# The norm's scale per token moved behind the matmul, with sums and root beside the first unit of each stage

## Chip, cores and metric

One core of a Trainium2 chip runs the whole program. The metric is the device time of one execution in microseconds (us).

## The reference, cut to what matters

One inference step of a two-layer decoder trunk for 592 tokens (64 sample tokens, 16 meta tokens, a prompt of 512), D_MODEL 1024, D_FF 4096. Every sub-layer is preceded by a norm over the features:

```python
def _rmsnorm(x, g, eps=1e-6):
    xf = x.astype(jnp.float32)
    y = xf * lax.rsqrt(jnp.mean(xf * xf, axis=-1, keepdims=True) + eps)
    return (y * g.astype(jnp.float32)).astype(x.dtype)

def _sq_relu_mlp(x, w_up, w_down):
    return jnp.square(jax.nn.relu(x @ w_up)) @ w_down
...
        hp = hp + _sq_relu_mlp(_rmsnorm(hp, ln_ffn[l]), w_up[l], w_down[l])
        hs = hs + _sq_relu_mlp(_rmsnorm(hs, ln_ffn[l]), w_up[l], w_down[l])
```

(hp and hs are the prompt's and the samples' activations; the mixers stand behind a norm in the same way, and a final norm follows.) Layer 0's mixer has one input projection (24 column blocks of 128 and a small one of 140 columns), sparse attention and a gated delta rule side by side, and one output projection. Layer 1's mixer is the HGRN2 recurrence between an input projection (forget, query and gate, 24 blocks; values, 1024 columns) and an output projection. The norm's root is one number per token, so it can be applied to a product's columns as well as to the activations. In the MLP the square makes it a factor root squared on the hidden values, which again can wait until after the second product.

## The kernel before, in words

Activations lie feature-major: h, xn, x_hi and x_lo are eight tiles (k) of 128 features by 592 tokens. Weights come as units of 128x1024 (512 KB), 200 in all, through a ring of four slots that SP refills (`sp_weights`, L1944 on). Every product is made in split precision: ScalarE rounds a weight unit to w_hi (`act_w_hi`, L353), VectorE makes the rest, w_lo (`dve_w_lo`, L357); the activations are split in the same way (`act_x_hi`, L332; `dve_x_lo`, L339). `pe_unit` (L360 to 374) multiplies one unit: per tile k six matmuls of 296 columns, 48 in all, into two of four PSUM banks, so units alternate between two pairs of banks. A unit waits for its split weights and for the evacuation two units back. ScalarE and VectorE split unit j + 2 when unit j has ended.

The stages of units are: 24 of layer 0's input projection (`pe_even`, `act_even`, `dve_even`, L1405 to 1470, with the small product `pe_small`, L485, after the second unit, and the rotation of keys and queries, `pe_rope`, after units 1 to 6); attention and the delta rule; 8 of the output projection (`pe_dense`, `act_out`, `dve_out`); 64 of the first MLP (`pe_ffn`, `act_ffn`, `dve_ffn`: four steps of 8 up units and 8 down units); 24 of the odd layer's projection, evacuated by ScalarE (`act_dense`, L393); 8 of its values (`pe_values5`, L1515, tokens in rows, in all banks); the recurrence; 8 of its output projection; 64 of the second MLP; a last norm and the output's DMA.

A norm (number n, 0 to 4) stands ahead of each of the five stages of products or output. ScalarE squares tile k of h (`act_square`, L278) as soon as its residual is added, into one of two buffers; GpSimd (VectorE for n = 0) adds tiles 0 to 6 into rn (`add_squares`, L287, L290). `pe_norm` (L314) sums over features with a matrix of ones, four matmul instructions for rn and four for the last square. ScalarE takes logarithm and root (`act_root`, L301, L304). VectorE scales tile by tile (`dve_norm`, L322: h times the norm's weight times the root), alternating with x_lo, while ScalarE makes x_hi between them; the first unit takes each tile when it is there.

In the MLP VectorE evacuates: a maximum (L470) and a square (L472) for up units, `dve_residual` (L425: h plus the product) for down units and output projections.

The opening: SP's queue sends x in four parts of 592 KB, then four weight units; ScalarE's queue sends the constants (2046 KB, with the matrix of ones and the rotation tables), the vectors (57 KB, with the norms' weights) and the small product's weights (560 KB); GpSimd's queue sends the page table and the convolution's history. All engines wait for constants and vectors before they start.

Of the kernel before, what the change touches and what calls it, by code (L numbers as in the profile page):

```python
# [147 lines left out]
def hybrid_step(nc, x, consts, keep, at, w, wsmall, vecs, stconv, sdelta, shgrn, kvpages, ptab,  # L148
                y, krows, vrows, ikrows, convo_p, convo_s, delta_p, delta_s, hgrn_p, hgrn_s):
    ctx = ExitStack()  # L150
    with ctx:
# [59 lines left out]

        pages = region(B, NS * NPG, 3 * P).rearrange("p (s g) (a c) -> p s g a c", s=NS, a=3)
# [55 lines left out]
        def act_square(n, k):  # L268
            if n == 0:
                nc.scalar.wait_ge(sg(f"x_in{k * XIN // KT}"), 16)  # L270
            else:
                m0 = (Units.out_e, Units.odd - 8, M_OUT_O, UNITS - VUNITS - 8)[n - 1]
                nc.scalar.wait_ge(bank_free, m0 + k + 3)
# [6 lines left out]
        def add_squares(eng, n):  # L280
            for k in range(1, KT - 1):
                c = (KT - 2) * n + k
                eng.wait_ge(sg("norm_sq"), KT * n + k + 1)
                if k == 1:
                    if n:
                        eng.wait_ge(sg("x_f"), KT * n)
# [19 lines left out]
        def pe_norm(n):  # L306
# [3 lines left out]
            for last, v in enumerate((rn[:, :], sq[:, 1, :])):  # L310
                if last:
                    nc.tensor.wait_ge(sg("norm_sq"), KT * (n + 1))
                for e in range(2):
                    mm = nc.tensor.matmul(ps[:, 6 + e, 0:HALF], C("ones"), v[:, e * HALF:(e + 1) * HALF],  # L314
                                          start=(not last), stop=bool(last))
            mm.then_inc(sg("norm_mm"), 1)

        def dve_norm(n, dst):
            nc.vector.wait_ge(sg("norm_rt"), n + 1)
            for k in range(KT + 1):  # L320
                if k < KT:
                    ins = nc.vector.scalar_tensor_tensor(out=dst[:, k, :], in0=h[:, k, :],  # L322
                                                         scalar=vec[:, V_LN + 8 * n + k:V_LN + 8 * n + k + 1],
                                                         in1=rn[:, :], op0=ALU.mult, op1=ALU.mult)
                    ins.then_inc(sg("x_f"), 1)
                if k and n < 4:
                    dve_x_lo(dst, k - 1)


# [30 lines left out]
        def pe_unit(base, per, i, j, x, first=None):  # L360
# [5 lines left out]
            for k in range(KT):  # L366
                if first:
                    first(k)
                for a, b in ((wh, x[0]), (wh, x[1]), (wl, x[0])):
                    for e in range(2):  # L370
# [3 lines left out]
                                              stop=(k == KT - 1 and a is wl))  # L374
            mm.then_inc(w_used, 1)
# [8 lines left out]
        def pe_dense(groups, u0, n):  # L384
            with nc.tensor.Fori(0, groups) as i:
# [1852 lines left out]
```

## Time and profile before

| | us |
|---|---|
| median of 3 runs (1964.08 to 1965.65) | 1964.26 |
| the profiled execution | 1966.28 |
| its span, first to last instruction | 1964.5 |
| TensorE busy | 1763.5 (90%) |
| VectorE busy | 920.0 (47%) |
| ScalarE busy | 613.3 (31%) |
| GpSimd busy | 289.8 (15%) |
| mean granted TensorE clock, share of full | 0.924 |
| share of TensorE in the chain that ended last | 73% |

The profiled execution is one program run with the hardware profiler on; its span is what the rows below are times of, from the first instruction. "PE" is TensorE, "PEld" its weight load, "DVE" VectorE, "ACT" ScalarE, "POOL" GpSimd, "SP" SyncE. A busy share says nothing about waits: for these one reads what ended the idle time before an instruction.

### The profile page before, as it was taken

Reading aid. Unit: us, or ns where it says so; the run is one execution under the profiler, and the core shown is the slowest. Engines: PE = TensorE matmul, PEld = TensorE weight load, DVE = VectorE, ACT = ScalarE, POOL = GpSimd, SP = SyncE. Lnnn points to the kernel's source line nnn. Section 1 sums busy time; section 2 is a strip of 40 time slices with the busy share of each in tenths; the row PEclk is TensorE's granted clock in tenths of the full one; section 3 lists DMA queues with packets and bytes.
Section 4 is the critical chain, followed back from the end, with each engine's and each line's share of the span. In section 5 each row is a group of like instructions: output and inputs, shape, how many; then the busy total and the mean of one; then the engine's idle time right before and its main releaser. Section 6 shows DMA issues by size and latency. Waiting matters only on the chain.

```text
span 1964.5 us, 33346 instructions
## 1 busy us (share of the span) xinstructions
PE 1763.5 (90%) x13834; PEld 1657.1 (84%) x13834; DVE 920.0 (47%) x1471; ACT 613.3 (31%) x980; POOL 289.8 (15%) x339
## 2 busy tenths in 40 slices
PE   3989877797798999999998999777879999999996
PEld 3989745796688999999998998556668999999996
DVE  4489967642245434343434111268743634444342
ACT  3234544221233212121223232466532322222121
POOL 0136300241010000000020000267702000000001
PEclk9999979796799999999999999867769999999998
DMA  6122310000021222222221222201112222222221
GB/s 173 56 63 65 120 33 7 38 2 1 33 92 58 82 78 82 77 83 78 82 77 62 86 75 75 66 34 59 47 55 86 64 77 82 78 81 79 79 81 49
DMA packets 37166, 132.41 MB, mean 67 GB/s; under 512 B 4816, under 2 KB 7712, under 8 KB 36560
## 3 DMA queue, kind: packets, MB, share of 16 engines
q1 hardware_dynamic: 35552, 122.11, 19.9%
q0 software_dynamic: 1088, 6.25, 0.9%
q10 hardware_dynamic: 432, 2.73, 0.5%
q8 instruction: 67, 1.10, 0.2%
q14 instruction: 27, 0.22, 0.0%
HBM read 119.90 MB, written 10.84 MB: 67 GB/s over the span
## 4 chain that ended last, share of the span: by engine, by line
PE 73%; DVE 15%; ACT 5%; issue 3%; POOL 1%; DMA 1%; DVEq 0%; SPq 0%; ACTq 0%; POOLq 0%
PE ps L371 57%; PE ps L1515 3%; DVE arena L1114 1%; DVE arena L595 1%; DVE best L1116 1%; PE ps L786 1%; DVE xn L322 1%; PE ps L807 1%; DVE x_lo L339 1%; DMA h<-in_x 1%; PE ps L805 1%; DVE wsp L357 1%; PE ps L904 1%; ACT rn L301 1%; DVE arena L1780 1%
## 5 line engine op out<-in xcount | busy, mean ns | idle before, releaser
L371 PE MATMUL ps<-x_hi,wsp 128*128 128x296 f32 x4096 | 745.8, 303 | 29.9 <-DVE x_lo L339 27.3
L371 PEld LDWEIGHTS ps<-x_hi,wsp 128*128 128x128 f32 x4096 | 622.2, 191 | 38.9 <-issue 21.3
L353 ACT ACTIVATE wsp<-ring 128x1024 fp32r<-128x1024 f32 x200 | 211.9, 1061 | 906.8 <-PE ps L371 877.6
L371 PE MATMUL ps<-x_lo,wsp 128*128 128x296 f32 x2048 | 449.3, 301 | 0.0
L371 PE MATMUL ps<-hid,wsp 128*128 128x296 f32 x3072 | 421.1, 299 | 0.0
L371 PEld LDWEIGHTS ps<-hid,wsp 128*128 128x128 f32 x3072 | 420.3, 189 | 0.0
L357 DVE TENSOR_TENSOR wsp<-ring,wsp 128x1024 fp32r<-128x1024 f32 x200 | 249.2, 1247 | 217.1 <-ACT wsp L353 216.5
L371 PEld LDWEIGHTS ps<-x_lo,wsp 128*128 128x128 f32 x2048 | 337.9, 191 | 0.0
L425 DVE TENSOR_TENSOR h<-h,ps 128x592 f32<-128x592 f32 x80 | 61.8, 772 | 327.6 <-PE ps L371 327.6
L470 DVE TENSOR_SCALAR sq<-ps 128x592 f32<-128x592 f32 x64 | 49.6, 775 | 204.5 <-PE ps L371 204.5
L287 POOL TENSOR_TENSOR rn<-sq 128x592 f32<-128x592 f32 x4 | 7.6, 1909 | 857.6 <-ACT sq L278 857.6
L457 ACT ACTIVATE hid<-sq 128x592 fp32r<-128x592 f32 x64 | 44.9, 702 | 34.6 <-DVE sq L472 34.6
L1515 PE MATMUL ps<-wsp,x_hi 128*128 128x512 f32 (+1 forms) x160 | 50.1, 394 | 1.8 <-ACT arena L393 1.8
L290 POOL TENSOR_TENSOR rn<-rn,sq 128x592 f32<-128x592 f32 x20 | 37.9, 1893 | 92.7 <-ACT sq L278 92.7
L1695 POOL TENSOR_TENSOR xn<-xn 128x256 f32<-128x256 f32 (+2 forms) x56 | 50.6, 903 | 3.8 <-ACT xn L1636 3.6
L472 DVE TENSOR_TENSOR sq<-sq 128x592 f32<-128x592 f32 x64 | 49.6, 775 | 2.2
L480 DVE TENSOR_TENSOR hid<-sq,hid 128x592 fp32r<-128x592 f32 x64 | 49.2, 768 | 0.0
L1717 POOL TENSOR_TENSOR xn<-xn 128x64 f32<-128x64 f32 (+2 forms) x24 | 11.9, 522 | 249.9 <-DVE xn L1738 249.9
L1743 DVE TENSOR_TENSOR sq<-sq,arena 128x256 f32<-128x256 f32 (+2 forms) x38 | 27.3, 719 | 43.8 <-ACT sq L1636 43.7
L1696 POOL TENSOR_TENSOR xn<-xn 128x256 f32<-128x256 f32 (+2 forms) x56 | 47.0, 840 | 0.0
L807 PE MATMUL ps<-arena,sq 128*128 128x128 f32 (+1 forms) x216 | 39.4, 278 | 0.0
L1515 PEld LDWEIGHTS ps<-wsp,x_hi 128*128 128x128 f32 (+1 forms) x160 | 28.7, 180 | 10.0 <-issue 2.0
(318 smaller groups left out, 1896.5 us busy)
## 6 DMA issues: line engine op xcount, KB each, us to landing
ring<-in_w SPq DMA_DIRECT2D x200, 512.0 KB, 3.6
arena<-in_shgrn SPq DMA_DIRECT2D x8, 512.0 KB, 3.6
out_hgrn_s<-arena SPq DMA_DIRECT2D x8, 512.0 KB, 2.9
arena<-in_kvpages SPq DMA_DIRECT2D x16, 192.0 KB, 2.4
h<-in_x SPq DMA_DIRECT2D x4, 592.0 KB, 17.8
out_y<-xn SPq DMA_DIRECT2D x1, 2368.0 KB, 7.0
arena<-in_sdelta POOLq DMA_DIRECT2D x1, 2048.0 KB, 8.4
out_delta_s<-arena POOLq DMA_DIRECT2D x1, 2048.0 KB, 7.2
```

What stands on the lines that cost most here:

```text
L353: nc.scalar.activation(wsp[:, j % 2, 0, :], ring[:, j % SLOTS, :], ACT.Copy).then_inc(w_hi, 1)
L357: nc.vector.tensor_tensor(wsp[:, j % 2, 1, :], ring[:, j % SLOTS, :], wsp[:, j % 2, 0, :].bitcast(F32), ALU.subtract).then_inc(w_lo, 1)
L371: mm = nc.tensor.matmul(ps[:, 2 * (j % 2) + e, 0:HALF], a[:, k * P:(k + 1) * P], b[:, k, e * HALF:(e + 1) * HALF], start=(k == 0 and a is ...
L425: nc.vector.tensor_tensor(pairs(h[:, k, :]), pairs(h[:, k, :]), ps[:, 2 * (j % 2):2 * (j % 2) + 2, 0:HALF], ALU.add).then_inc(bank_free, 1)
L457: nc.scalar.activation(hid[:, 0, j, :], sq[:, j % 2, :], ACT.Copy).then_inc(sg("hid_hi"), 1)
L470: nc.vector.tensor_scalar(pairs(sq[:, j % 2, :]), pr, 0.0, None, ALU.max).then_inc(bank_free, 1)
L472: nc.vector.tensor_tensor(sq[:, j % 2, :], sq[:, j % 2, :], sq[:, j % 2, :], ALU.mult)\
L480: nc.vector.tensor_tensor(hid[:, 1, j, :], sq[:, j % 2, :], hid[:, 0, j, :].bitcast(F32), ALU.subtract).then_inc(sg("hid_split"), 1)
L807: mm = nc.tensor.matmul(bank(3 + 2 * (m % 2), R, R)[:, hd], P1[m % 2][0:R, hd, 0:R], Tt[t][0:R, hd, 0:R], start=True, stop=True)
L1515: mm = nc.tensor.matmul(ps[0:ROWS[t], v_bank(a, t), :], x[:, 2 * q + k, c], w_[:, 512 * k:512 * (k + 1)], start=(q == 0 and k == 0 and x i ...
L1695: nc.gpsimd.tensor_tensor(d_[:, :, 0, :], mid, k_[:, :, 0, :], ALU.add)
L1696: nc.gpsimd.tensor_tensor(d_[:, :, 1, :], c_[:, :, 1, :], mid, ALU.subtract)\
```

## The change

The tiles that a stage multiplies are h times the norm's weight (`act_h_hi`, `dve_h_lo`), without the root. The root is applied when products are evacuated. Sums (`pe_norm`) and root (`act_norm`) stand behind the first unit of the stage.

- Ahead of an MLP (norms 1 and 3): `pe_out` releases each tile of x_hi and x_lo during the last unit of the output projection (`x_free`), so that tiles 0 to 6 are made during it, and tile 7 after the last residual. The up units are evacuated as before; the down units are multiplied by the root squared into `scaled`, and added to h in a second operation (`dve_ffn_residual`).
- Ahead of the odd layer (norm 2): the tiles are made in the last eight down units of the MLP. VectorE evacuates all 24 units and multiplies by the root; ScalarE applies Silu to groups 1 and 2 in place. For the values, where tokens lie in rows, `pe_norm(2)` adds ten matmuls with one column (20 instructions), ScalarE roots the result into `rcol`, and it is the scale of the values' evacuation.
- Norm 0: the tiles are made from x as it arrives. The first three units (`U_RAW`) run on them and are scaled by VectorE at evacuation. VectorE then makes the normalised activations (`dve_norm`) behind the first unit's evacuation, and both engines split those after the third unit, for the rest of the stage. The small product follows the third unit rather than the second, in banks 6 and 7 rather than 4 and 5.
- The opening's DMAs: SP's queue sends x part 0, weight unit 0, x part 1, weight unit 1, x parts 2 and 3, weight units 2 and 3. ScalarE's queue sends the vectors first, the constants after tile 1's x_hi, the small product's weights after tile 3's.
- The last norm (4) stays as it was, with the root on the activations.

```diff
@@ act_norm, pe_norm
         def act_norm(n):
+
             nc.scalar.wait_ge(sg("norm_mm"), n + 1)
-            act_root(rn[:, :], ps[:, 6:8, 0:HALF], 1.0 / D, C("eps"), "norm_ln", "norm_rt")
-            if n < 4:
-                for k in range(KT):
-                    act_x_hi(xn if n else xn0, k, "x_f", KT * n + k + 1)
+            if n in (0, 4):
+                act_root(rn[:, :], ps[:, 6:8, 0:HALF], 1.0 / D, C("eps"), "norm_ln", "norm_rt")
+                return
+            nc.scalar.activation(pairs(rt), ps[:, 6:8, 0:HALF], ACT.Ln, scale=1.0 / D, bias=C("eps"))\
+                .then_inc(sg("norm_ln"), 1)
...
+            nc.scalar.activation(rt, rt, ACT.Exp, scale=-0.5 if n == 2 else -1.0).then_inc(sg("norm_rt"), 1)
...
+            if n == 2:
+                for t in range(NT):
+                    c = slice(COL0[t], COL0[t] + ROWS[t])
+                    for last, v in enumerate((rn[:, :], sq[:, 1, :])):
+                        mm = nc.tensor.matmul(ps[0:ROWS[t], 6, HALF + t:HALF + t + 1], v[:, c], C("ones")[:, 0:1],
+                                              start=(not last), stop=bool(last), skip_group_check=True)
@@ the tiles
+        def act_h_hi(n, k):
+
+            if n == 0:
+                nc.scalar.wait_ge(sg(f"x_in{k * XIN // KT}"), 16)
+            else:
+                if n % 2 and k < KT - 1:
+                    nc.scalar.wait_ge(sg("x_free"), (KT - 1) * (n // 2) + k + 1)
+                act_h_ready(n, k)
+            nc.scalar.activation(x_hi[:, k, :], h[:, k, :], ACT.Copy, scale=ln_scale(n, k)).then_inc(sg("x_hi"), 1)
+
+        def dve_h_lo(n, k):
+            split_count[0] += 1
+            nc.vector.wait_ge(sg("x_hi"), split_count[0])
+            nc.vector.scalar_tensor_tensor(out=x_lo[:, k, :], in0=h[:, k, :], scalar=ln_scale(n, k),
+                                           in1=x_hi[:, k, :].bitcast(F32), op0=ALU.mult, op1=ALU.subtract)\
+                .then_inc(sg("x_split"), 1)
@@ output projection
+        def act_out(u0, norm):
+            for j in range(GROUP - 1):
                 act_w_hi(u0, GROUP, 0, j + 2)
                 act_square(norm, j)
+            for k in range(KT - 1):
+                act_h_hi(norm, k)
+            act_w_hi(u0, GROUP, 0, GROUP + 1)
+            act_h_hi(norm, KT - 1)
+            act_square(norm, KT - 1)
...
+        def dve_ffn_residual(n, base, i, j, k):
+
+            nc.vector.wait_ge(w_used, base + STEP * i + j + 1)
+            nc.vector.tensor_tensor(pairs(scaled[:, j % 2, :]), ps[:, 2 * (j % 2):2 * (j % 2) + 2, 0:HALF],
+                                    pairs(rt), ALU.mult).then_inc(bank_free, 1)
+            nc.vector.wait_ge(bank_free, base - VUNITS * n + STEP * i + j + 3)
+            nc.vector.tensor_tensor(h[:, k, :], h[:, k, :], scaled[:, j % 2, :], ALU.add).then_inc(sg("h_new"), 1)
+
+        def dve_out(u0, norm):
             for j in range(GROUP):
+                if j == GROUP - 1:
+                    for k in range(KT - 1):
+                        dve_h_lo(norm, k)
                 dve_residual(u0, GROUP, 0, j, j)
+                if j == GROUP - 1:
+                    dve_h_lo(norm, j)
                 dve_w_lo(u0, GROUP, 0, j + 2)
@@ layer 0's input projection
             for u in range(U_EVEN):
-                pe_unit(Units.even, U_EVEN, 0, u, X_SPLIT, x_tiles(0) if u == 0 else None)
-                if u == 1:
+                pe_unit(Units.even, U_EVEN, 0, u, X_SPLIT, x_tiles(u // U_RAW) if u in (0, U_RAW) else None)
+                if u == 0:
+                    nc.tensor.wait_ge(const_in, 16)
+                    pe_norm(0)
+                if u == U_RAW - 1:
                     pe_small()
                     nc.tensor.wait_ge(sg("small_ev"), NT)
...
+        def dve_even_raw(u):
+
+            if u == 0:
+                nc.vector.wait_ge(sg("norm_rt"), 1)
+            nc.vector.wait_ge(w_used, u + 1)
+            nc.vector.tensor_tensor(pairs(proj[:, EVEN_TILES[u], :]), ps[:, 2 * (u % 2):2 * (u % 2) + 2, 0:HALF],
+                                    pairs(rn[:, :]), ALU.mult).then_inc(bank_free, 1)
+            if u == 0:
+                dve_norm(0, xn0)
+            if u == U_RAW - 1:
+                for k in range(KT):
+                    dve_x_lo(xn0, k)
```

## Rows read from the trace of the kernel before

**Rows 1.** The page, chain that ended last, shares of the span by line.

```profile
PE ps L371 57%; PE ps L1515 3%; DVE arena L1114 1%; DVE arena L595 1%; DVE best L1116 1%; PE ps L786 1%; DVE xn L322 1%; PE ps L807 1%; DVE x_lo L339 1%; DMA h<-in_x 1%; PE ps L805 1%; DVE wsp L357 1%; PE ps L904 1%; ACT rn L301 1%; DVE arena L1780 1%
```

**Rows 2.** Chain of waits at norm 2: start us, us, what.

```profile
1038.37 1.58 DVE xn L322 x2
...
1049.39 10.67 PE ps L371 x76
```

**Rows 3.** Timeline at norm 1: start us, us, engine, line, operation, tiles, count [idle before, releaser].

```profile
602.76 1.16 PE L314 MATMUL ps<-rn,cst 128*128 128x296 f32 x4
...
602.96 0.77 DVE L425 TENSOR_TENSOR h<-h,ps 128x592 f32<-128x592 f32 x1 [4.18 <-PE ps L371]
...
609.82 0.83 DVE L322 SCALAR_TENSOR_TENSOR xn<-h,vec,rn 128x592 f32<-128x592 f32 x1
...
610.05 0.83 PE L371 MATMUL ps<-x_hi,wsp 128*128 128x296 f32 x2 [4.07 <-DVE x_lo L339]
...
610.68 0.70 ACT L332 ACTIVATE x_hi<-xn 128x592 fp32r<-128x592 f32 x1 [0.84 <-DVE xn L322]
...
620.51 0.77 DVE L470 TENSOR_SCALAR sq<-ps 128x592 f32<-128x592 f32 x1 [1.18 <-PE ps L371]
...
627.08 0.77 DVE L470 TENSOR_SCALAR sq<-ps 128x592 f32<-128x592 f32 x1 [3.16 <-PE ps L371]
```

**Rows 4.** Timeline at norm 2.

```profile
1033.80 0.77 DVE L425 TENSOR_TENSOR h<-h,ps 128x592 f32<-128x592 f32 x1 [4.18 <-PE ps L371]
...
1051.43 1.06 ACT L353 ACTIVATE wsp<-ring 128x1024 fp32r<-128x1024 f32 x1 [2.05 <-PE ps L371]
```

**Rows 5.** Stretch at norm 1: length, busy (instructions) per engine, TensorE clock, DMA share, GB/s.

```profile
609.00:615.90 6.90, 5.85 (x24) 5.88 (x25) 6.88 (x11) 3.58 (x6) 0.00 (x0) 0.51 0.00 0
```

**Rows 6.** Timeline of the start: norm 0 on TensorE, end of the first unit.

```profile
25.69 2.31 PE L314 MATMUL ps<-rn,cst 128*128 128x296 f32 x4 [25.69 <-DVE rn L290]
...
27.80 1.66 PE L314 MATMUL ps<-sq,cst 128*128 128x296 f32 x4
...
45.35 1.06 ACT L353 ACTIVATE wsp<-ring 128x1024 fp32r<-128x1024 f32 x1 [2.05 <-PE ps L371]
```

**Rows 7.** Timeline of TensorE in the delta rule: matmuls with one column, and what follows.

```profile
346.81 1.03 PE L687 MATMUL ps<-cst,gates 128*128 128x1 f32 x8
347.70 1.14 PE L694 MATMUL ps<-cst,gates 128*128 128x128 f32 x8
```

**Rows 8.** Timeline at the values product.

```profile
1203.70 0.67 PE L1515 MATMUL ps<-wsp,x_hi 128*80 128x512 f32 x2 [1.79 <-ACT arena L393]
```

**Rows 9.** Timeline of VectorE in the down units of the first MLP.

```profile
680.65 1.23 DVE L357 TENSOR_TENSOR wsp<-ring,wsp 128x1024 fp32r<-128x1024 f32 x1 [0.32 <-ACT wsp L353]
686.12 0.77 DVE L425 TENSOR_TENSOR h<-h,ps 128x592 f32<-128x592 f32 x1 [4.24 <-PE ps L371]
```

**Rows 10.** Source view of x's DMAs (L1957, four of them, issued 0.8 to 2.2 us).

```profile
DMA to landing us min/median/max: 9.6/17.8/21.3
```

**Rows 11.** Stretches of the start (columns as rows 5); DMA queues from 6 to 8 us.

```profile
5.00:10.00 5.00, 0.00 (x0) 0.00 (x0) 0.00 (x0) 0.00 (x0) 0.89 (x1) 1.00 0.98 389
10.00:15.00 5.00, 0.00 (x0) 0.00 (x0) 0.00 (x0) 1.28 (x1) 0.00 (x0) 1.00 1.07 137
...
25.00:30.00 5.00, 3.77 (x8) 2.39 (x8) 2.90 (x3) 4.14 (x5) 0.00 (x0) 1.00 0.77 273
...
q10 hardware_dynamic: 38, 0.62, 78.2%
q1 hardware_dynamic: 40, 0.19, 24.6%
```

**Rows 12.** Timeline of the start: small product, rotation, splits of weights after units.

```profile
51.66 9.70 PE L492 MATMUL ps<-arena 128*80 128x140 f32 x80
...
61.81 1.26 PE L543 MATMUL ps<-arena,cst 128*128 128x296 f32 x4 [0.47 <-DVE tokm L512]
...
77.30 1.06 ACT L353 ACTIVATE wsp<-ring 128x1024 fp32r<-128x1024 f32 x1 [1.06 <-PE ps L371]
```

More of the change, by code:

```diff
@@ L358, in dve_w_lo, with pe_unit @@
                                     ALU.subtract).then_inc(w_lo, 1)
-        def pe_unit(base, per, i, j, x, first=None):
+        def pe_unit(base, per, i, j, x, first=None, free=False):
             nc.tensor.wait_ge(w_lo, base + per * i + j + 1)
@@ L374, in pe_unit @@
                                               stop=(k == KT - 1 and a is wl))
+                if free and k < KT - 1:
+                    mm.then_inc(sg("x_free"), 1)
             mm.then_inc(w_used, 1)
@@ L391, in act_evacuate @@
             if not isinstance(i, int):
-                nc.scalar.wait_ge(const_in, 32)
+                nc.scalar.wait_ge(const_in, 16)
             nc.scalar.activation(pairs(dst), ps[:, 2 * (j % 2):2 * (j % 2) + 2, 0:HALF], func).then_inc(bank_free, 1)
-        def act_dense(groups, u0, dst, func, more=True):
-            def step(i, last):
-                for j in range(GROUP):
-                    if j < GROUP - 2 or not last:
-                        act_w_hi(u0, GROUP, i, j + 2)
-                    act_evacuate(u0, i, j, dst[:, GROUP * i + j, :], func)
-            with nc.scalar.Fori(0, groups if more else groups - 1) as i:
-                step(i, False)
-            if not more:
-                step(groups - 1, True)
@@ L407, in dve_w_los, with act_silu_unit @@
-        def dve_w_los(groups, u0, more=True):
-            def step(i, last):
-                for j in range(GROUP):
-                    if j < GROUP - 2 or not last:
-                        dve_w_lo(u0, GROUP, i, j + 2)
-            with nc.vector.Fori(0, groups if more else groups - 1) as i:
-                step(i, False)
-            if not more:
-                step(groups - 1, True)
-        def act_out(u0, norm):
+        def act_silu_unit(base, i, j, dst):
+            m0 = base + 3 if isinstance(i, int) else base + 3
+            nc.scalar.wait_ge(bank_free, m0 + GROUP * i + j)
+            nc.scalar.activation(dst, dst, ACT.Silu)
@@ L458, in step @@
                     if squares and j >= GROUP:
+                        if more and j == STEP - 1:
+                            act_h_hi(2 * n + 2, j - GROUP)
                         act_square(2 * n + 2, j - GROUP)
-            with nc.scalar.Fori(0, STEPS - 1) as i:
+                        if more and j < STEP - 1:
+                            act_h_hi(2 * n + 2, j - GROUP)
+            step(0, False)
+            with nc.scalar.Fori(1, STEPS - 1) as i:
                 step(i, False)
@@ L481, in step @@
                                                 ALU.subtract).then_inc(sg("hid_split"), 1)
-            ffn_steps(nc.vector, step, more)
+            step(0, False)
+            with nc.vector.Fori(1, STEPS - 1) as i:
+                step(i, False)
+            step(STEPS - 1, not more)
         def pe_small():
@@ L1957, in _ @@
                 sp.dma_start(h[:, c, :], x[:, c, :]).then_inc(sg(f"x_in{i}"), 16)
-            for s in range(SLOTS):
+                if i < 2:
+                    sp.dma_start(ring[:, i, :], w[i]).then_inc(w_in[i], 16)
+            for s in range(2, SLOTS):
                 sp.dma_start(ring[:, s, :], w[s]).then_inc(w_in[s], 16)
```

191 lines of the change are left out of this document (125 added, 66 removed).

## Prediction

> **What bounds the kernel now.** I read the chain that ended last first, by line: 57% of the span is the one line with which TensorE multiplies a weight unit (L371) [rows 1]. That does not say what a norm costs, so next comes the chain in order of time, and the timeline, where a norm stands between two stages. Between the first MLP and the odd layer's projection [rows 2] the chain leaves TensorE: the last square, the norm's matmuls, logarithm, root, and then, from 1038.37, 16 VectorE operations that scale and split tile by tile, until TensorE bounds itself again at 1049.39. The timelines give the price of each of these places, from the moment a unit ends to the end of the next unit: 602.96 to 620.51 [rows 3], 1033.80 to 1051.43 [rows 4], and the first pattern once more ahead of the second MLP (three such places in all). That is 17.55, 17.6 and 17.55 us for one unit of work that takes 6.56 us in the steady stream (620.51 to 627.08) [rows 3]. So some 11 us are lost at each of three places, and a part of that is the half clock after the gap: granted 0.51 from 609.0 to 615.9 [rows 5]. The start is a fourth place: its first unit ends at 45.35 [rows 6].
>
> **The change at the three inner norms.** The tiles that TensorE reads become h times the norm's weight, without the root, so they can be made while the unit before still runs. After the attention output projection (and likewise after the odd layer's): let E be the end of its last unit. ScalarE makes x_hi of tiles 0 to 6 behind TensorE's release of each tile (one per 0.82 us, an eighth of 6.56), at 0.70 us each, VectorE x_lo at 0.83 (the rows of the same two shapes, at 610.68 and 609.82 [rows 3]); tile 6 is ready at about E + 1. Then come the last residual (0.77), x_hi of tile 7 (0.70) and x_lo (0.83): E + 3.4. TensorE wants tile 7 after seven eighths of the unit, at E + 5.7. The unit's weights were split a unit earlier. So TensorE goes on at E without a gap, with 2.3 us to spare, and the clock does not fall. The norm's eight matmul instructions stay on its path behind this unit: four take 1.16 us [rows 3], eight 2.35. Gain: 17.55 - 6.56 - 2.35 = **8.6 us, twice** (17.2). Late next is nothing: the root runs on ScalarE behind the second unit, is wanted first by the ninth unit, and only holds one hidden tile back by 1.5 us where VectorE has 3.16 us idle per unit [rows 3].
>
> At the odd layer's projection the same holds (there x_hi is free early, since the down units read the hidden tiles). It adds ten matmuls with one column for the root per token, 20 instructions. The nearest row is eight matmul instructions with one column in 0.89 us (346.81 to 347.70) [rows 7], 0.11 each: 2.2 us; below that nothing excludes half, above it the 0.29 of the 296-column form would give 5.8. I take 2.2. Gain 17.6 - 6.55 - 2.35 - 2.2 = **6.5 us** (3 to 7.6).
>
> VectorE now evacuates all 24 odd units (0.77) and ScalarE no longer. Before, TensorE waited 1.79 us at the values product [rows 8], for ScalarE to split a weight unit and then evacuate; now VectorE evacuates at once: 0.85. Gain **0.9 us**.
>
> In the down units VectorE multiplies and adds in place of one add: 0.77 more, 64 times. Its work per unit was 0.77 + 1.23 [rows 9]; it becomes 2.8, with the next x_lo in the last eight 3.6, under 6.56. Weight units are split 0.8 us later, in a slack above 3 us, and SP refills the ring behind that with four slots. Cost zero, covered by TensorE's unit. At the very end there is no cover: the last square waits for multiply and add, and the closing norm for it one VectorE operation later. Loss **0.8 us**.
>
> **The start** is the uncertain term. Here the first three units run on the raw tiles, then VectorE and ScalarE make the normalised ones for the rest. What paces it is the last quarter of x. It was issued at 2.2 and landed 21.3 us later, at 23.5 [rows 10]; SP's queue now sends two weight units ahead of it, and ScalarE's queue sends the constants later, no longer ahead. The bytes of the whole opening are the same, and the stream was slow from 10 to 20 us (137 GB/s after 10, 389 before that) [rows 11]. Ends: x, two weight units and the vectors, 3.5 MB, at 389 GB/s from 2 us on give 11 us; if x were to come last of all, 28, when the opening's stream thins out (273 GB/s from 25 to 30 [rows 11]). I keep 23, since it is still the same mix of queues that carries them.
>
> From there, with rows: two x_hi, a square between them, an x_lo: 3.0; the last tile at half clock 1.5; end of unit 1 at 27.5. Norm at half clock 3.8 (25.69 to 29.45 [rows 6]): 31.3. Second unit 37.9, rotation 1.26 [rows 12], third unit 45.7. Then a serial piece that was not there: weight split on both engines 1.06 + 1.23 [rows 9, 12], evacuation 0.77, eight x_lo at 0.77: 54.8. The small product has two banks, so three of its five parts wait for VectorE behind that: from 55.4, 1.9 each, 61.1. It was 9.70 for all five in one piece [rows 12]. TensorE idles from 49.4 to 55.4 here, longer than the 4.07 us before the half clock of [rows 3, 5], so I charge that again: 3 us. Last copy, rotation 1.25, fourth unit 6.56: 72.3. Before, the fourth unit ended at 77.30 [rows 12]. Gain **5.0 us**, ends -1 (x at 28 or later) and +15 (x at 15 and full clock). What VectorE does from there on (top-k rounds, convolution) is the same list, so the shift should last.
>
> I charge no ScalarE table load: the change adds no function that the kernel did not call at the same place, and ScalarE's root lies beside a unit everywhere but at the very end.
>
> **Sum:** 17.2 + 6.5 + 0.9 - 0.8 + 5.0 = 28.8. The profiled execution took 1966.28 us with a span of 1964.5; minus 28.8 is 1937.5. It lies 2.0 above the median of the three runs, 1964.26, against which I forecast **1935.5**.
>
> **Rivals.** (a) *The constants still hold x up.* In the 2 us from 6 to 8, ScalarE's queue moved 38 packets and SP's 40, but 0.62 MB against 0.19 [rows 11]: packet for packet, and the constants' are 16 KB (0.62 MB / 38). If they take their share ahead of the last quarter, only two weight units (1.05 MB, 2.6 us at 0.4 MB per us) are left behind it and x lands at about 25.5; with a second half-clock stretch of 3 us the start gains nothing: 1940.5. For: the packet counts. Against: x is issued from 0.8 us on, the constants from about 9. The Trainium skill, "DMA: Bandwidth & Descriptors", section on queues, rings and completion order, states it as a rule: each DMA engine alternates between the queues that have work, a whole packet at a time. By that rule the order in SP's queue alone cannot bring x forward, and the packet counts above agree.
>
> (b) *TensorE stays at full clock and x comes sooner*, by 15 to 18: the start gains 11 to 14, 1928. For: without the constants in the first 8 us x has the stream to itself. Against: half clock followed the gap in [rows 5]; with half clock in the small product the start is worth 5, without it 8. The Trainium skill, "TensorE: Matmul & The Clock Gate", on HAM oscillation, says that a wait between bursts sends TensorE back to half clock for the next burst; it speaks against this change wherever that opens a new gap, as it does in the small product, and for it at the three inner norms.
>
> (c) *The cover at the inner norms is too thin*: tile 7 comes more than 2.3 us later than I worked out (a queued ScalarE weight split, a slow release of the tiles), and each of three places gives back 3 us: 1944.5.
>
> (d) *Slower:* VectorE becomes the bound of the MLP units. Its down unit grows by 0.77, and a weight unit that is split late stops TensorE two units on. The point from which it decides is a split over 3.3 us late; then each of the 64 down units would have to lose 28.8 / 64 = 0.45 us to undo the rest; at 0.55 each it ends at 1970.5. For it speaks only that VectorE gets more work; against it 4.24 us idle per down unit [rows 9].
>
> (e) *It does not do what it says:* TensorE still waits for the root, because the first evacuation needs it and the banks are two. Then only the time of making the tiles moves; some 1963. Against: the MLP's first evacuation is a maximum and needs no root, and in the odd layer the root is there 4 us before the third unit.
>
> **Chances.** Forecast 0.60 (own range 1931 to 1940), (a) 0.17, (b) 0.12, (c) 0.06, (d) 0.02, (e) 0.03. The likeliest is 1935.5. The range 1926 to 1944 takes in (a) and (b), the ends of the start and of the one-column matmuls, and a few us for half-clock stretches that fall elsewhere. A measurement of this kernel can tell about 0.2% (3.9 us) from none: faster 0.95, same 0.03, slower 0.02.
>
> **What would show it.** In the timeline: no TensorE gap after the last output-projection unit and after the last down unit, and full granted clock through both; from unit end to the end of the next unit and norm 8.9 us, 11.1 at the odd layer; VectorE's down unit at 2.8 us with 3.4 idle. At the start: x landing at 21 to 25, a TensorE gap of 6 us inside the small product, the fourth unit ending near 72. It is wrong if a gap stands before tile 7, if VectorE ends a chain inside the MLPs, or if the stage from the fourth unit to the attention grew.

## The result and the profile after

| | before | after |
|---|---|---|
| median, us (4 runs each, side by side) | 1964.83 | 1948.11 (1947.07 to 1949.4) |
| profiled execution, us | 1966.28 | 1947.07 |
| span, us | 1964.5 | 1945.3 |
| granted TensorE clock | 0.924 | 0.923 |

The ratio is 0.9919, with an interval of 0.9907 to 0.9932. The change gains 16.7 us between the medians and 19.2 between the two spans, where 28.8 were forecast. The median of 1948.1 lies outside the range of 1926 to 1944. Rows below are of the profiled executions, so the 19.2 is what they have to add up to.

The page of the kernel after, its parts 1, 3 and 4: busy time by engine, the queue from which engines get their instructions (packets, MB, share), and the chain's lines.

```profile
PE 1759.6 (90%) x13854; PEld 1659.7 (85%) x13854; DVE 981.5 (50%) x1546; ACT 615.1 (32%) x981; POOL 285.7 (15%) x339
...
q8 instruction: 101, 1.65, 0.4%
...
PE ps L418 59%; PE ps L1643 3%; DVE arena L1213 2%; DVE best L1215 1%; DVE arena L694 1%; PE ps L885 1%; PE ps L906 1%; DMA h<-in_x 1%; PE ps L904 1%; DVE wsp L404 1%; PE ps L1003 1%; DVE arena L1909 1%; PE ps L959 1%; PE ps L340 1%; ACT rn
```

The weight unit's line (now L418) went from 57% to 59% of a shorter span [rows 1]: the chain left TensorE less often. VectorE grew by 61.5 us, of which the second operation of 64 down units is 49.6, and that cost nothing, as forecast. The line of q8 is something that no step of the forecast looked at: 101 instruction packets of 16 KB, where the page of before has 67 of them (`q8 instruction: 67, 1.10, 0.2%`).

**Norm 1, as forecast.** The chain of waits from 590 to 620, then ScalarE's and VectorE's timelines there:

```profile
589.93 16.27 PE ps L418 x119
606.20 1.99 PE ps L340 x8
608.19 11.89 PE ps L418 x87
```

```profile
599.73 1.06 ACT L400 ACTIVATE wsp<-ring 128x1024 fp32r<-128x1024 f32 x1
602.65 0.79 ACT L368 ACTIVATE x_hi<-h,vec 128x592 fp32r<-128x592 f32 x1 [1.86 <-DVE h L493]
...
614.85 1.06 ACT L400 ACTIVATE wsp<-ring 128x1024 fp32r<-128x1024 f32 x1 [6.29 <-PE ps L418]
```

```profile
595.53 6.40 DVE L373 SCALAR_TENSOR_TENSOR x_lo<-h,vec,x_hi 128x592 fp32r<-128x592 f32 x7
601.86 0.76 DVE L493 TENSOR_TENSOR h<-h,ps 128x592 f32<-128x592 f32 x1
603.48 0.83 DVE L373 SCALAR_TENSOR_TENSOR x_lo<-h,vec,x_hi 128x592 fp32r<-128x592 f32 x1 [0.86 <-ACT x_hi L368]
```

The chain is on TensorE all through. In [rows 5] the clock was 0.51; the same stretch of time, now in the second unit, has 1.00:

```profile
609.00:615.90 6.90, 6.90 (x53) 6.90 (x52) 1.72 (x3) 1.05 (x2) 0.00 (x0) 1.00 0.25 78
```

From the end of the last output-projection unit (599.67, one unit of 6.56 behind the end of the unit before at 593.11; ScalarE takes up the next split at 599.73) to the end of the second unit are 15.18 us, against 24.12 (602.96 to 627.08 in [rows 3]): 8.9 gained. Tile 7 was ready at 604.31, 4.6 after the unit's end; 3.4 was forecast, 5.7 was the limit. VectorE worked off the other x_lo first and came to the residual at 601.86. The margin was 1.1 us, not 2.3.

**Where the gain is lost again.** The table subtracts the times at which units ended. An end is read from the weight split with which ScalarE follows it:

| up to the end of | before | after | gain | forecast for this piece |
|---|---|---|---|---|
| fourth unit | 77.30 | 73.31 | 4.0 | +5.0 |
| sixth of the output projection's eight units | 589.89 | 586.61 | 3.3 | 0 |
| second unit of the first MLP | 627.08 | 614.85 | 12.2 | +8.6 |
| second unit of the odd layer | 1057.98 | 1040.31 | 17.7 | +6.5 |
| values and recurrence (first weight split behind them) | 1455.75 | 1435.36 | 20.4 | +0.9 |
| second unit of the second MLP | 1539.87 | 1510.58 | 29.3 | +8.6 |
| first unit of its second step | 1638.27 | 1608.72 | 29.6 | 0 |
| first unit of its third step | 1743.23 | 1717.35 | 25.9 | 0 |
| first unit of its fourth step | 1848.25 | 1828.23 | 20.0 | 0 |
| its third last unit | 1933.53 | 1913.51 | 20.0 | 0 |
| span | 1964.5 | 1945.3 | 19.2 | -0.8 |

At 1608.72 the change is worth 29.6 us, as much as the forecast has up to there (28.8 and the 0.8 of the end). Then 9.5 go, at two places: at the turns from step to step. TensorE's timeline at the first:

```profile
1699.76 7.12 PE L418 MATMUL ps<-hid,wsp 128*128 128x296 f32 x51
1708.86 0.54 PE L418 MATMUL ps<-x_hi,wsp 128*128 128x296 f32 x2 [1.97 <-issue]
1709.23 0.43 PE L418 MATMUL ps<-x_lo,wsp 128*128 128x296 f32 x2
1709.50 0.57 PE L418 MATMUL ps<-x_hi,wsp 128*128 128x296 f32 x3
1711.55 0.30 PE L418 MATMUL ps<-x_hi,wsp 128*128 128x296 f32 x1 [1.48 <-issue]
```

And at the second, 109 us on, with the clock there (columns as [rows 5]):

```profile
1817.67 0.67 PE L418 MATMUL ps<-x_hi,wsp 128*128 128x296 f32 x2 [1.95 <-issue]
...
1820.46 0.41 PE L418 MATMUL ps<-x_hi,wsp 128*128 128x296 f32 x1 [0.90 <-issue]
```

```profile
1817.80:1824.60 6.80, 5.90 (x24) 5.79 (x25) 0.67 (x1) 0.00 (x0) 0.00 (x0) 0.51 0.26 82
```

The waits end on "issue": no semaphore, no tile, no weight was late. From hid to x_hi is where TensorE's program jumps back from the end of one step of the MLP to the start of the next. The queues from 1700 to 1712 show three instruction packets, `q8 instruction: 3, 0.05, 1.5%`; two of them start at 1706.2 and 1709.3, some 2.5 us ahead of the two restarts. In the kernel before no such packet stands between 1700 and 1930. The kernel before runs its four steps in one loop. The kernel after writes the first step out, because that one takes its tiles as they come and has the norm in it, and loops over the other three. Twice a loop of three jumps back, and twice there is a stall; the second one is accompanied by half clock.

So the theory for the experiments is that the missing 9.5 us are code and not data. The rival is that the second MLP has a late transfer or tile that the trace does not show.

### The profile page after: what moved, and what is told of

It is laid out like the page before. It is cut to its first block, busy times and chain, and to the rows that moved or that the text cites. A ratio compares the mean times of both kernels' runs of the same rounds, so it can differ in the third digit from the quotient of the medians.

```text
span 1945.3 us, 33322 instructions
## 1 busy us (share of the span) xinstructions
PE 1759.6 (90%) x13854; PEld 1659.7 (85%) x13854; DVE 981.5 (50%) x1546; ACT 615.1 (32%) x981; POOL 285.7 (15%) x339
## 4 chain that ended last, share of the span: by engine, by line
PE 75%; DVE 13%; ACT 5%; issue 3%; POOL 2%; DMA 1%; SPq 0%; DVEq 0%; ACTq 0%; POOLq 0%
PE ps L418 59%; PE ps L1643 3%; DVE arena L1213 2%; DVE best L1215 1%; DVE arena L694 1%; PE ps L885 1%; PE ps L906 1%; DMA h<-in_x 1%; PE ps L904 1%; DVE wsp L404 1%; PE ps L1003 1%; DVE arena L1909 1%; PE ps L959 1%; PE ps L340 1%; ACT rn L327 0%
## 5 line engine op out<-in xcount | busy, mean ns | idle before, releaser
L418 PE MATMUL ps<-x_hi,wsp 128*128 128x296 f32 x4096 | 745.3, 303 | 34.2 <-DVE wsp L404 13.3
L418 PEld LDWEIGHTS ps<-x_hi,wsp 128*128 128x128 f32 x4096 | 622.7, 191 | 38.3 <-DVE wsp L404 21.5
L418 PE MATMUL ps<-x_lo,wsp 128*128 128x296 f32 x2048 | 449.9, 301 | 0.0
L418 PE MATMUL ps<-hid,wsp 128*128 128x296 f32 x3072 | 420.9, 299 | 0.0
L418 PEld LDWEIGHTS ps<-hid,wsp 128*128 128x128 f32 x3072 | 420.0, 188 | 0.0
L418 PEld LDWEIGHTS ps<-x_lo,wsp 128*128 128x128 f32 x2048 | 338.2, 192 | 2.6 <-issue 2.6
L499 DVE TENSOR_TENSOR arena<-ps,arena 128x592 f32<-128x592 f32 x64 | 49.5, 774 | 221.5 <-PE ps L418 221.5
L474 DVE TENSOR_TENSOR arena<-ps,arena 128x592 f32 x24 | 18.6, 774 | 107.4 <-PE ps L418 99.2
L502 DVE TENSOR_TENSOR h<-h,arena 128x592 f32<-128x592 f32 x64 | 49.6, 776 | 2.2
L563 DVE TENSOR_TENSOR sq<-sq 128x592 f32<-128x592 f32 x64 | 49.6, 775 | 2.2
L1872 DVE TENSOR_TENSOR sq<-sq,arena 128x256 f32<-128x256 f32 (+2 forms) x38 | 27.5, 723 | 43.3 <-ACT sq L1765 43.2
## 6 DMA issues: line engine op xcount, KB each, us to landing
h<-in_x SPq DMA_DIRECT2D x4, 592.0 KB, 11.6
```

The source lines that it names most:

```text
L418: mm = nc.tensor.matmul(ps[:, 2 * (j % 2) + e, 0:HALF], a[:, k * P:(k + 1) * P], b[:, k, e * HALF:(e + 1) * HALF], start=(k == 0 and a is ...
L499: nc.vector.tensor_tensor(pairs(scaled[:, j % 2, :]), ps[:, 2 * (j % 2):2 * (j % 2) + 2, 0:HALF], pairs(rt), ALU.mult).then_inc(bank_free, 1)
L502: nc.vector.tensor_tensor(h[:, k, :], h[:, k, :], scaled[:, j % 2, :], ALU.add).then_inc(sg("h_new"), 1)
L563: nc.vector.tensor_tensor(sq[:, j % 2, :], sq[:, j % 2, :], sq[:, j % 2, :], ALU.mult)\
```

## The experiments

All kernels are the kernel after with one edit, unless said otherwise.

**1. Both MLPs of TensorE without a loop.**

```diff
             step(0)
-            with nc.tensor.Fori(1, STEPS) as i:
+            for i in range(1, STEPS):
                 step(i)
```

> The changed kernel with TensorE's program for both MLPs written out in full (four steps each) in place of one written-out step and a loop over three. Same work, same waits. Theory A (instruction loading): in the changed kernel the loop of the second MLP is loaded anew at each turn (16 KB instruction packets go on to 1922 us, where before they end at 1615), and TensorE waits at its two jumps back; straight code is loaded ahead without a wait, as in the first stage. Then the second MLP loses its 9.5 us no more: about 1938.5 us, no idle time with releaser 'issue' inside the MLPs. Theory B (the loss in the second MLP comes from late weights or from VectorE's added work): no change, 1948.

Measured: 1935.91 us (1934.75 to 1936.72), ratio 0.9857 (0.9841 to 0.9874), span 1932.9. The waits of TensorE's own program between 1600 and 1930 are gone from the table of waits; in the kernel after they are these two lines of it (engine, line, what for: us in all, times, longest):

```profile
PEld ps L418 <- issue: 7.0, 4, 2.2
PE ps L418 <- issue: 6.3, 4, 2.0
```

From the second unit of the second MLP to its third last it took 392.8 us, the kernel after 402.9, the kernel before 393.7 (and 393.6 in experiments 6 to 8, which are straight too). It fetches more instructions (107 packets, one every 17 us to the end) and waits for none, as in this line of its queues from 1600 to 1900:

```profile
q8 instruction: 17, 0.28, 0.4%
```

So it is not the fetching that costs but the jump to code that has to be fetched. Of the 12.4 us between the spans 10.1 are in that stage; 2.2 are in the attention (the first weight split behind it at 530.87 against 533.05), and they are not the edit's: see the recurrence in the next section.

**2. The written-out first step in the kernel before,** nothing else.

```diff
-            with nc.tensor.Fori(0, STEPS) as i:
-                ...
+            def step(i):
+                ...
+            step(0)
+            with nc.tensor.Fori(1, STEPS) as i:
+                step(i)
```

> The kernel before, and of the change only the shape of TensorE's MLP program: the first step written out, then a loop over three. No norm is moved. Theory A (code alone): if the mere extra step ahead of the loop makes a loop load anew, the second MLP loses some 9.5 us here too, 1974 us. Theory A' (code, but by where the loop lies in the program): may be 1964.5 or 1974, as the lengths of code ahead differ from the changed kernel's; the instruction packets tell. Theory B (VectorE's work or weights): 1964.5, no packets beyond those of before.

Measured: 1965.23 us (10 runs), ratio 1.0005 (0.9995 to 1.0014), 79 packets, no "issue" wait in the MLPs' loops, 393.7 us for the stage. The extra step alone, on which the expectation leaned, does not do it. Its loop of three was fetched once and then jumped back for nothing; so was the loop of the first MLP in the kernel after, with this line for 820 to 1020 (q14 is another queue, and q8 has none):

```profile
q14 instruction: 1, 0.01, 0.0%
```

One and the same loop is free in one place and costs 9.5 us in another.

**3. No one-column matmuls.** The values' root per token is read from other columns, so the values come out otherwise.

```diff
-            if n == 2:
-                for t in range(NT):
-                    ...   # 10 matmuls with one column
```

> The changed kernel without the ten matmuls with one column at the odd layer's norm (ScalarE takes other numbers as the values' scale, so the layer's values are another thing). Theory A (they cost their own 2.0 us, and the half clock that follows them, 1032.7 to 1036.1, another 1.8): 3.8 us less, 1944.3, full clock through the odd layer's first units. Theory B (the half clock comes from the norm's eight matmuls): 2.0 less, 1946.1, half clock still there.

Measured: 1933.44 us (1932.99 to 1937.71), ratio 0.985 (0.9834 to 0.9867). At the norm it did as foreseen: TensorE's timeline and the clock there, first of the kernel after, then of this one.

```profile
1029.86 0.24 PE L346 MATMUL ps<-cst,rn 128*80 128x1 f32 x2
...
1031.67 0.36 PE L346 MATMUL ps<-cst,sq 128*128 128x1 f32 x2
1031.89 0.52 PE L418 MATMUL ps<-x_hi,wsp 128*128 128x296 f32 x2
...
1033.71 1.19 PE L418 MATMUL ps<-x_hi,wsp 128*128 128x296 f32 x4
```

```profile
1032.00:1036.00 4.00, 4.00 (x21) 4.00 (x21) 1.89 (x2) 1.82 (x6) 0.00 (x0) 0.61 0.00 0
```

```profile
1025.60:1034.80 9.20, 9.20 (x63) 8.72 (x63) 1.91 (x2) 2.90 (x8) 0.00 (x0) 1.00 0.28 97
```

The twenty instructions take 2.03 us (1029.86 to 1031.89), then four matmuls take 1.19 in place of 0.71: half clock, though TensorE did not pause. From the end of the first unit to that of the second it is 12.18 us with them and 8.56 without, so they cost 3.6, of which 1.6 is clock. The half clock does not always follow them. In experiment 9, whose program is the same up to there, the first line below is its clock from 1024 to 1038, the second that of the kernel after; from unit end to unit end it took 10.66 us:

```profile
1024.00:1038.00 14.00, 14.00 (x103) 13.48 (x102) 2.98 (x4) 3.34 (x8) 0.00 (x0) 1.00 0.25 76
1024.00:1038.00 14.00, 14.00 (x91) 13.48 (x90) 3.83 (x4) 3.38 (x8) 0.00 (x0) 0.88 0.18 52
```

The other seven kernels that have them at this place (after, 1, 4, 5, 6, 7 and 11) took 12.2. The rest of the gain I did not foresee: the second MLP's stall was gone too (393.6 us, 82 packets). The code in front of that loop was shorter, and nothing in the loop was changed.

**4. The small product's copies between the x_lo tiles,** not behind all eight.

```diff
                 for k in range(KT):
                     dve_x_lo(xn0, k)
+                    if k in (2, 4, 6):
+                        small_copy(k // 2 - 1, dlink)
```

> The changed kernel with VectorE's first three copies of the small product put between the x_lo tiles (after tiles 2, 4 and 6) in place of behind all eight. Theory A (TensorE's gap of 5.3 us in the small product and the half clock behind it cost the start 7 us, as the five parts take 16.7 us where they took 9.7): the fourth unit ends about 6 us sooner, 67 in place of 73.3, and the end with it: 1942. Theory B (VectorE's list from there on is the bound, so what is won at the small product is waited for later): the fourth unit is sooner, the end within 1 us of 1948.

Measured: 1942.72 us (1940.89 to 1945.48), ratio 0.9891 (0.9875 to 0.9908). TensorE's timeline of the small product, kernel after and this kernel:

```profile
47.81 3.97 PE L591 MATMUL ps<-arena 128*80 128x140 f32 x32
57.09 7.43 PE L591 MATMUL ps<-arena 128*128 128x140 f32 x48 [5.30 <-DVE tokm L611]
```

```profile
47.83 3.98 PE L591 MATMUL ps<-arena 128*80 128x140 f32 x32
53.68 5.99 PE L591 MATMUL ps<-arena 128*128 128x140 f32 x48 [1.88 <-DVE tokm L609]
```

The gap falls by 3.4 us and the piece behind it by 1.4, since TensorE stays at full clock; the fourth unit ends at 68.47 rather than 73.31. The second MLP took 405.6 us here, 2.6 more than in the kernel after, though TensorE's program is the same. The waits are 1.1 us longer in all (7.4 for 6.3), and half clock followed the first stall as well, as in this row, where the kernel after has 0.70:

```profile
1706.57 1.19 PE L418 MATMUL ps<-x_hi,wsp 128*128 128x296 f32 x4
```

**5. Only the first MLP without a loop.**

> The changed kernel with only the first MLP written out on TensorE; the second keeps the loop that lost 9.5 us in the changed kernel. The loop's code is the same, it only lies some 3000 instructions later in the program. Theory A1 (a loop of this length is loaded anew or not by where its code lies, as the run without the one-column matmuls suggests, where 40 instructions fewer ahead of it stopped it): the second MLP may lose 9.5 us or nothing; if nothing (about 1936.5), place alone decides. Theory A2 (in that run it was the missing work, not the missing code): the loss stays, 1945 to 1948, with instruction packets on to 1920 us.

Measured: 1948.61 us (2 runs), ratio 0.992 (0.99 to 0.994). First MLP: 413.3 us from its second unit to the odd layer (612.38 to 1025.65), as in the kernel after (614.85 to 1028.13). The second: 406.0, with

```profile
PE ps L418 <- issue: 6.0, 3, 2.2
```

The loss sits in the second MLP alone. The first one's code is longer here by some 3,000 instructions of TensorE (1,536 matmuls and as many weight loads), and that did not cure it, so it is not enough to move the loop; where it is moved to counts (experiments 9 and 10).

**6 and 7. What held x up.** Both with straight MLPs, so compare with experiment 1. In 6 GpSimd's DMA of the convolution's history (144 KB, in runs of three values) waits for x's last part; in 7 the constants are issued after tile 6's x_hi.

```diff
# 6
+            pool.wait_ge(sg(f"x_in{XIN - 1}"), 16)
             pool.dma_start(hist[:, :, :, 0:CONV_W - 1], stconv)
# 7
-                if k == 1:
+                if k == KT - 2:
                     act.dma_start(cst[:, :], consts)
```

> The changed kernel with both MLPs straight, and GpSimd's DMA of the convolution's history (144 KB, first used after 100 us) issued when the last part of x has landed. Theory A (its small pieces are what makes the opening's stream slow from 8 to 22 us, so x's last part lands at 25.8 though it is ahead in its queue): x lands at 14 to 17, the first unit ends at 19 to 22, and the end comes 9 us sooner: 1927. Theory B (the constants hold x up, in packets of 16 KB): x lands about 1 to 3 us sooner, 1934.

> The changed kernel with both MLPs straight, and the constants (2046 KB) issued after tile 6 in place of tile 1, with x's last part landed. Theory A (history): x's last part lands little sooner, 22 to 24, and the first norm then waits for the constants, some 6 us after that: first unit's end sooner by 2 to 3 us, second unit's later; end 1938 or more. Theory B (constants): x's last part lands at 18 to 20, and the first norm ends no later than before; 1933.

Measured: 6, 1928.55 us (1928.08 to 1928.8), ratio 0.9817 (0.9801 to 0.9834); 7, 1939.06 us (2 runs), ratio 0.9871 (0.9852 to 0.9891). ScalarE's timeline shows x's last quarter landing and the next weight split, which in the first two stands at the end of the first unit and in 7 at the constants' landing; kernel after, 6, 7:

```profile
25.83 0.79 ACT L368 ACTIVATE x_hi<-h,vec 128x592 fp32r<-128x592 f32 x1 [3.25 <-DMA h<-in_x]
...
30.99 1.06 ACT L400 ACTIVATE wsp<-ring 128x1024 fp32r<-128x1024 f32 x1 [2.52 <-PE ps L418]
```

```profile
18.61 0.79 ACT L368 ACTIVATE x_hi<-h,vec 128x592 fp32r<-128x592 f32 x1 [0.15 <-DMA h<-in_x]
...
23.02 1.06 ACT L400 ACTIVATE wsp<-ring 128x1024 fp32r<-128x1024 f32 x1 [1.76 <-PE ps L418]
```

```profile
18.40 0.79 ACT L368 ACTIVATE x_hi<-h,vec 128x592 fp32r<-128x592 f32 x1 [1.37 <-DMA h<-in_x]
...
29.69 1.06 ACT L400 ACTIVATE wsp<-ring 128x1024 fp32r<-128x1024 f32 x1 [8.64 <-DMA cst<-in_consts]
```

And the stream from 10 to 15 us, in experiment 1 and in 6, last number GB/s:

```profile
10.00:15.00 5.00, 4.11 (x16) 4.11 (x17) 4.82 (x6) 3.75 (x6) 0.00 (x0) 1.00 1.06 262
```

```profile
10.00:15.00 5.00, 3.88 (x16) 3.88 (x17) 4.82 (x6) 3.98 (x6) 0.00 (x0) 1.00 1.03 437
```

Either transfer out of the way brings x to 18.5, so neither theory has it alone. The constants are not worth moving, since the first norm needs their matrix of ones: ScalarE waits 8.6 us for them, TensorE 7.1. Without the history, which GpSimd first reads at about 116 us, the same 16 DMA engines, busy all the time in both, move 437 GB/s rather than 262. The gain was 7.5 us at the sixth unit of the output projection (576.92 for 584.42) and 7.4 between the medians. The Trainium skill, "DMA: Bandwidth & Descriptors", section on why small descriptors are slow, gives a fixed overhead per packet and a fixed amount of metadata per descriptor for it; that pieces this small depress the whole stream is in line with these two rows, though no run here separates the causes. The rule of the same page of the Trainium skill, section on queues, rings and completion order, that queues alternate packet by packet, agrees too: in 7 x came sooner although its own queue was not touched.

**8. The one-column matmuls behind the 24 units,** ahead of the values (with straight MLPs).

> The changed kernel with both MLPs straight, and the ten matmuls with one column put behind the odd layer's 24 units, ahead of the values, where TensorE waits 1.08 us for an evacuation anyway; ScalarE's logarithm and root of them stand in the values' stage. Theory A (half clock followed them because 2 us of them stood with the norm's own): the odd layer's first units run at full clock, 1.6 us won there, 1.0 hidden in the wait: 1933.3. Theory B (they bring the half clock wherever they stand): 1.6 us lost at the values product in place of at the odd layer, 1934.9.

Measured: 1937.51 us (1936.66 to 1939.76), ratio 0.9867 (0.985 to 0.9883), that is 1.6 more than experiment 1 rather than less. The odd layer's second unit came 8.55 us after the first, at full clock. But the half clock went with the columns (experiment 1 has 1.00 in the same window):

```profile
1182.00:1189.00 7.00, 7.00 (x26) 5.35 (x25) 0.07 (x1) 0.00 (x0) 0.00 (x0) 0.79 0.22 75
```

The values' first matmul came 2.2 us sooner than in experiment 1, after 3.0 before the columns, and behind the half clock 0.6 were left. ScalarE now loads tables of 1.28 us three times there, but TensorE's table of waits for the values has no line for it. The rest went in the recurrence: its end is 1.8 us later than in experiment 1 (1434.95 against 1433.13). I did not show why.

**9 and 10. Code, moved without touching the loop.** In 9 the kernel after gets 25 one-column matmuls (about 100 instructions) ahead of the second output projection. Experiment 10 is experiment 3 with ten of them there.

```diff
         def pe_out(u0, n):
+            for f in range(25 if u0 == Units.out_o else 0):   # 10 in the other
+                nc.tensor.matmul(ps[:, 4, HALF + 4:HALF + 5], C("ones"), C("ones")[:, 0:1], start=True, stop=True)
```

> The changed kernel with 25 matmuls of one column (some 100 TensorE instructions, their results unused) ahead of the second output projection, where TensorE waits 6.4 us anyway. The second MLP's loop is the same code and does the same work, it only lies 100 instructions later. Theory A1 (where the loop's code lies decides): the loss of 9.5 us may go; if so, about 1938.5 and no instruction packets from about 1700 to 1920 us. Theory A2 (whatever lies ahead, this form of program loses it): 1948, packets as in the changed kernel.

> The changed kernel without the one-column matmuls at the odd layer's norm (ScalarE takes other numbers as the values' scale), and with ten such matmuls (results unused) ahead of the second output projection instead: the same count of instructions ahead of the second MLP's loop as in the changed kernel. Theory A1 (place): the loop is loaded anew again and loses 9.5 us, 1943. Theory A2 (it was the missing work that cured it): 1933.5 as in the run without them.

Measured: 9, 1939.42 us (2 runs), ratio 0.9867 (0.9849 to 0.9885); 10, 1945.08 us (2 runs), ratio 0.9896 (0.9878 to 0.9914). 9 does more work than the kernel after and is 8.7 us faster, 1.5 of it at the odd layer's norm (experiment 3); 10 puts back into the fast version of experiment 3 nothing but a few instructions far ahead of the loop, and is 11.6 slower. Stage of the second MLP: 393.6 and 406.1 us. The table of waits of 10:

```profile
PEld ps L418 <- issue: 8.3, 4, 2.3
PE ps L418 <- issue: 7.6, 4, 2.1
```

The table of 9 has no such line. Instruction packets in all: 83 in 9, near the 82 of experiment 3, and 101 in 10, as in the kernel after. The loop's place in the program decides, and a late tile or transfer is excluded as the cause.

**11. The parts together:** straight MLPs, history behind x, copies of the small product between the tiles (one ahead of them, then after tiles 1, 3 and 6).

> The changed kernel with three edits together: both MLPs straight on TensorE, GpSimd's history DMA behind x's last part, and VectorE's copies of the small product between the x_lo tiles (one before them, then after tiles 1, 3 and 6). If the three gains add up (12.2, 7.4 and some 6 us; the first two are in the 1928.55 already measured): 1922. If VectorE's list in layer 0's stage takes some of it back: 1923 to 1928.

Measured over five rounds: 1921.19 us (1917.95 to 1922.35) beside 1965.15 (9 runs) of the kernel before, ratio 0.9771 (0.9758 to 0.9785). That is 27 us under the kernel after. The three gains between medians, 12.2, 7.4 and 5.4 (experiments 1, 6, 4), sum to 25.0; the third was measured with a stall 2.6 us longer than that of the kernel after, which is no longer there. The fourth unit's end fell from 73.31 to

```profile
56.77 1.06 ACT L400 ACTIVATE wsp<-ring 128x1024 fp32r<-128x1024 f32 x1 [12.54 <-PE ps L418]
```

## Why the prediction was right or wrong

By its own steps, each against the gain between the two spans:

- *The two norms of the MLPs, 8.6 each:* 8.9 each. The mechanism is right to the row: no gap, full clock, eight matmuls on the path (1.99 for 2.35: the two rows of 1.16 start 0.98 apart). The cover was thinner than worked out, 1.1 us instead of 2.3, and enough. Rival (c) did not happen.
- *The odd layer's norm, 6.5:* 5.4. The one-column matmuls were sized right (2.03 for 2.2). The half clock behind them, 1.6 us, stood nowhere in the sum; I looked for half clock only behind gaps.
- *Values, 0.9:* 0.7. TensorE's wait fell from 1.79 [rows 8] to 1.08.
- *The end, -0.8:* -0.8, the last line of the table of gains. The timeline at both places:

```profile
1185.61 0.67 PE L1643 MATMUL ps<-wsp,x_hi 128*80 128x512 f32 x2 [1.08 <-DVE arena L474]
...
1927.38 0.78 DVE L502 TENSOR_TENSOR h<-h,arena 128x592 f32<-128x592 f32 x1
...
1928.94 1.26 PE L340 MATMUL ps<-sq,cst 128*128 128x296 f32 x4 [1.41 <-ACT sq L281]
```

- *The start, 5.0:* 4.0 at the fourth unit, 3.3 by the output projection. x landed at 25.8, which is rival (a)'s landing, not 23, and so rival (b) did not happen; but rival (a)'s price, a start worth nothing, did not follow. The first unit ended 3.5 later than in my list (30.99 for 27.5), and the pieces after it were cheaper by 2.5: norm and second unit 9.5 for 10.4, third unit 7.6 for 7.8, and from there to the fourth unit's end 25.2 for 26.6. In the last piece the gap in the small product was there as worked out (5.30 for 6); the half clock behind it, for which I had 3 us, cost 1.4 (7.43 against 5.99 in experiment 4).
- *Recurrence, 0:* +2.3. The same 2,384 matmul instructions were busy for 140.4 us at a mean granted clock of 0.68 before, and for 135.2 at 0.70 after. The gain is there again in the variants: values and recurrence took 257.2 to 257.3 us in the kernel after and in experiments 1, 3, 4, 5, 7, 9 and 11 and 258.7 to 258.8 in 6 and 10, against 260.4 before and 260.2 in experiment 2 (in 8 the columns stand there). What in the change brings it is open. The 2.2 us of the attention are another thing: from the end of the fourth unit to the sixth of the output projection it took 513.2 to 513.9 us in the kernel after and in 7, 8, 9 and 11, but 511.1 to 511.5 in 1, 3, 4, 5, 6 and 10, with the clock at 0.66 and 0.95 from 340 to 350 in the kernel after and in 1. These go with no edit, so 2 us between two of these kernels may be no more than that.
- *Down units, cost zero:* right as to data. VectorE's multiply and add lie beside TensorE's unit, VectorE is idle for 3.5 us ahead of each (221.5 over 64; 3.4 was forecast), and without the stall the stage takes what it took before (393.6 to 393.7), so rival (d) did not happen. Nor did (e).
- **The step that failed** is the one that closed the account of the MLP there: "Cost zero, covered by TensorE's unit". It prices what VectorE does and says nothing of what TensorE's own program does. That program was changed, from a loop of four steps to a written-out step and a loop of three, and this cost 9.5 us in the second MLP: four waits for instructions, 6.3 us, and a stretch of half clock from the third on. With it the sum would have been 19.3, against 19.2 measured; though that is closer than its parts, since the recurrence's 2.3 stands against the 1.7 missing at the start and the 1.1 at the odd layer. Between the medians it is 16.7 because the profiled execution was 1.0 below its median here and 1.5 above it before (1964.83; the forecast's 2.0 was against the 1964.26 of three runs).

The sum of what was measured: 3.3 + 8.9 + 5.4 + 0.7 + 2.3 + 8.9 - 9.5 - 0.8 = 19.2, the difference of the spans. Left out are 0.3 lost in the odd layer's other units and 0.3 won in the second MLP's first step.

What remains open: which relation of the loop's length and place keeps it loaded. The straight version, the moved ones and the loop of the kernel before show only that it can be either, at 9.3 to 12.5 us for the two jumps. One regularity stands in the instruction queue's packets. In the four kernels that stall (after, 4, 5 and 10) a packet starts 0.3 to 0.7 us before TensorE enters the second MLP's loop, and one 0.5 to 0.8 us before each jump back. In the loops of three turns that do not stall, the last packet before the entry is 7.1 to 15.9 us old. Why this decides, no run here shows. The 2.3 and 2.2 us of the recurrence and the attention are open too.

## What to carry to other kernels

A scale that is one number per token can be taken out of the path of a stage: the next stage's tiles are then ready while the last one runs, and at two such places this kernel gained the serial chain and the half clock behind it, 8.9 us each. Where the bound engine runs a large loop, count a change of its code among the costs: look at the instruction packets around each jump back and for waits that end on "issue", and write the loop straight if they are there. In an opening that is bound by its stream, look first for a transfer in tiny pieces that nobody needs yet.

## What the runs showed of the hardware that I had not expected

- A loop of TensorE may be fetched again at every turn, or once for all turns, depending on what stands ahead of it in the program: 393.6 or 402.9 to 406.1 us for the same stage. Straight code, fetched in one packet per 17 us, had none of these waits in the five kernels that have it in the second MLP (1, 6, 7, 8 and 11).
- Matmuls with one column, issued back to back for 2.03 us, were followed by half clock (0.61 from 1032 to 1036), although TensorE is shown busy all through. This was so in seven of the eight kernels with them at this place; in experiment 9 the clock stayed at 1.00. Moved elsewhere, they took it along (0.79 from 1182 to 1189).
- With a DMA of 144 KB in runs of three values the stream of all queues stood at 262 GB/s from 10 to 15 us, and at 437 without it: 7.4 us for some 2% of the 7.3 MB that the first 20 us of experiment 6 move (5.5 MB in experiment 1).
